# Moving the recurrent mixer and the index selection of a hybrid encoder block between the groups of its input projection

## The chip, the cores and the metric

The kernel runs on one core of a Trainium2 chip. The metric is device time in microseconds for one launch, the median of three runs. A separate execution was profiled, and all durations below come from it.

## What is computed

One block of a hybrid encoder, in float32, for 256 tokens of width 2048:

```
h = h + 0.5 * swiglu(rms_norm(h), w_gate, w_up, w_down)          # FFN 1, d_ff 5632
u = rms_norm(h) @ w_in
q, k, v, qi, ki, wi, rr, rk, rv, wd, ad, gd = split_columns(u)
attn = dsa_attention(rope(q), rope(k), v, rope(qi), rope(ki), wi)
rwkv = rwkv7_time_mix(rr, rk, rv, wd, ad, gd, ...)
h = h + concat([attn, rwkv]) @ w_out
h = h + 0.5 * swiglu(rms_norm(h), ...)                           # FFN 2
return rms_norm(h)
```

The attention has 8 heads of 128. An indexer scores every key (8 small heads, relu, weighted sum), keeps the 64 best of each query under a chunk-causal mask, and the softmax runs over those. The recurrent half has 16 heads of 64. For each head and each time step it does

```
sa = state @ a_t
state = state * w_t + sa b_t^T + v_t k_t^T
y_t = state @ r_t
```

followed by a normalisation within heads, a bonus term and a gate.

## The kernel before

**Projections.** Weights stream through four slots. One group is 256 rows by 512 columns of a weight matrix (512 KB). SP issues its load into `raw` once the slot's earlier group has been split. ACT copies it to the rounded high part `whi` (`split_hi`, L279), DVE subtracts to get the low part `wlo` (`split_lo`, L288), and TensorE multiplies high by high, low by high and high by low (`project_tokens`, L303, or `project_channels`, L631, in the input projection). A split waits until TensorE has used the group four places earlier. Every engine runs its own list in order, so an operation that stands between two splits delays the later one. The groups of the middle part are numbered from the start of the input projection: 0 to 7 are its small columns, 8 to 87 its ten chunks of 512 columns, eight groups each. The output projection has four chunks of eight groups.

**The mixer during the input projection.** `win_dve`, `win_act` and `win_pe` list the splits and matmuls of groups 8 to 87, with the elementwise preparation of the recurrent half placed between them: `in_out(c)` scales a finished chunk out of PSUM, `lerp` mixes each token with its predecessor, then come the decay (a cumulative sum and two exponentials), the key norm, and the transposes to token order. Two PSUM pairs (`psA`, `psB`) take the chunks in turn, the other two (`psT`, `psM`) the small rounds. A round is filled by TensorE and read by DVE or ACT; `fill`, `full`, `stored` are its semaphores.

**The mixer after the input projection.** `systems_*` and `rwkv_*` follow, all before the output projection:
1. Within each chunk of 64 tokens the recurrence is a triangular system. TensorE forms the systems (`bx`, `kx`, L1405), DVE masks them.
2. The 32 by 32 diagonal blocks go to DRAM and come back with one block per partition. DVE inverts them by substitution, 31 steps of two instructions (`tinv`, `subst`). The inverses go back over DRAM (L1549 to L1557), and TensorE combines them to 64 by 64 (L1446, L1454, with copies by ACT between).
3. The index scores and the selection of 64 keys on DVE (`scores_dve`: eight pairs of `max` and `match_replace` for each half of the queries, L866).
4. `akv`, `sa0` and the state maps `gt` (L1432, L1468), then the scan over four chunks: solution `sa` (L1488), output `ys` (L1508, L1509), next state `st` (L1517, L1518), each read by DVE or ACT before the next. Logits, softmax and attended values (L943, L952, L961) stand between the scan's rounds.
5. The normalisation (L1354, L1345, L1338), bonus and gate, then the high and low parts for the output projection.

The weight buffers `raw`, `whi`, `wlo` hold mixer tensors in this part (`bx` lies in `whi`, `kx` in `wlo`, `att` in `raw`), so no weights can be split meanwhile. The residual `x` stays in SBUF throughout.

Of the kernel before, what the change touches and what calls it, by code (L numbers as in the profile page):

```python
# [17 lines left out]
F32 = mybir.dt.float32  # L18
# [5 lines left out]
P = 128  # L24
# [73 lines left out]
def build(nc, a, out):  # L98
    with ExitStack() as ctx:
# [48 lines left out]
        ar = at("ar", [P, 2, NT, S], arena, 0)  # L148
        kk, r = ar[:, 0, :, :], ar[:, 1, :, :]
        k, v = at("k", [P, NT, S], arena, 2), at("v", [P, NT, S], arena, 3)  # L150
        temp = at("temp", [P, 5, S], arena, 7)
        qk = at("qk", [P, 10, S], arena, plus=61 * KB)
        vals = at("vals", [P, TB, S], arena, plus=71 * KB)
        qi = at("qi", [P, 5, S], arena, plus=73 * KB)
        lora = at("lora", [P, 2, S], arena, plus=78 * KB)
        lora_w = at("lora_w", [P, RW], arena, plus=80 * KB)
        lora_g = at("lora_g", [P, RW], arena, plus=84 * KB)
        small_tok = at("small_tok", [P, TB, 320], arena, 5)
        mix_hi_at = (at("mix_hi0", [P, NT, S], arena, 0, dt=F32R), at("mix_hi1", [P, NT, S], arena, 1, dt=F32R))
        mix_lo_at = (at("mix_lo0", [P, NT, S], arena, 6, dt=F32R), at("mix_lo1", [P, NT, S], arena, 4, dt=F32R))  # L160
        rows_of = at("rows_of", [P, TB, P], arena, 5, 4 * KB)
        token_scale = sb("token_scale", [P, S])
        widx_scale = sb("widx_scale", [P, TB])
        widx = sb("widx", [P, TB, IDX_HEADS])

        att = (at("att0", [P, AH, P], raw, 1, 4 * KB), at("att1", [P, AH, S], raw, 0))
        turned = at("turned", [P, AH, S], raw, 0)
        relu = (at("relu0", [P, IDX_HEADS, P], stage, 0), at("relu1", [P, IDX_HEADS, S], raw, 0))
        prob_t = at("prob_t", [P, TB, AH, P], xl, 1)
        score = at("score", [P, TB, S], arena, 7)  # L170
        top8 = at("top8", [P, 8], arena, 7, 2 * KB)
        top = [at(f"top{i}", [P, 3 * AH], arena, 7, 2 * KB + 64 + 96 * i) for i in range(TB)]

        ksq = at("ksq", [P, NT, S], arena, 3)
        sw = at("sw", [P, NT, S], arena, 4)
        pdec = at("pdec", [P, NT, S], arena, 4)
        lsum = at("lsum", [P, NT, S], arena, 5)
        pinv = at("pinv", [P, NT, S], arena, 5)
        bonus = at("bonus", [P, NT, S], arena, 5)
        iclr = at("iclr", [P, NT, S], arena, 6)  # L180
        gate = at("gate", [P, NT, S], xh, 1)
        hstat = at("hstat", [P, 3, S], stage, plus=4 * KB)
        ka1 = sb("ka1", [P, NT])
        pend = sb("pend", [P, NT * NCHUNK, 1])

        a_tok = at("a_tok", [P, TB, RW], arena, 3)
        v_tok = at("v_tok", [P, TB, RW], arena, 4)
        b_tok = at("b_tok", [P, TB, RW], arena, 0)
        k_tok = at("k_tok", [P, TB, RW], arena, 6)
        bx = at("bx", [P, 2 * RH, 2, C], whi)  # L190
        kx = at("kx", [P, 2 * RH, 2, C], wlo)
        tt_all = at("tt_all", [P, 2 * RH, C], arena, 2)
        nsys = at("nsys", [P, 1024], arena, 10)
        tinv = at("tinv", [P, 1024], arena, 10, 4 * KB)
        subst = at("subst", [P, 1024], stage, 0, 4 * KB)
        t_plain = at("t_plain", [P, 2 * RH, 32], raw, 1)
        xm = at("xm", [P, 2 * RH, 32], arena, 9, KB)
        akv = at("akv", [P, TB, RW], xl, 1)
        sa0 = at("sa0", [P, TB, RW], stage)
        gt = at("gt", [P, TB, RW], arena, 3)  # L200
        state = at("state", [P, NT, C], arena, 10)
        sdec = at("sdec", [P, NT, C], arena, 10, 2 * KB)
        sa = at("sa", [P, RW], arena, 10, 4 * KB)
        y = at("y", [P, NT, S], arena, 2)
        ysq = at("ysq", [P, NT, S], arena, 3)
# [41 lines left out]
        a_rest = sem("a_rest")  # L247
        lora_landed = sem("lora_landed")
        round_full = sem("round_full")
        round_read = [sem(f"round_read{i}") for i in range(4)]  # L250
        sys_stored = sem("sys_stored")
# [96 lines left out]

        def turn_x(f, c):
# [5 lines left out]
            if c >= 2 or f:  # L355
                nc.tensor.wait_ge(xl_ready, DC * f + c - 1)
            if f == 0 and c == 1:
                nc.tensor.wait_ge(params_ready, 1)
            ps = (psT, psM)[c % 2]
# [6 lines left out]
        def x_hi(f, c):  # L366
# [3 lines left out]
            ps = (psT, psM)[c % 2]  # L370
# [6 lines left out]
        def x_lo(f, c):  # L377
            nc.vector.wait_ge(xh_ready, DC * f + c + 1)
            ps = (psT, psM)[c % 2]
# [148 lines left out]
        def ffn_pe(f, base):  # L528
# [11 lines left out]
            def chunk(n, first):  # L540
# [3 lines left out]
                for j in range(GD):  # L544
                    if first and j % 2 == 0:
                        if f == 0:
                            for q in ((0, 1), (2,), (3,), ())[j // 2]:
                                turn_x(0, q)
                        elif j == 2:
                            turn_x(2, 3)  # L550

                        nc.tensor.wait_ge(xl_ready, 4 * (2 * f) + j // 2 + 1)
                    project_tokens(psA, xh, xl, base, n, PER, j, j * KT, j == 0, j == GD - 1)
                if not first:
                    turn(n - 1)
                elif f == 0:
                    turn_params()
# [1260 lines left out]
```

## Time and profile before

| | |
|---|---|
| median of 3 runs | 2056.07 us (2054.09 to 2060.73) |
| profiled execution | 2050.65 us, its span 2048.8 us |
| TensorE / DVE / ACT / POOL busy | 1965.0 / 1070.0 / 835.4 / 8.2 us |
| mean granted clock of TensorE | 0.968 |
| DMA | 349.37 MB, mean 171 GB/s |

Busy time is the union of an engine's instructions; matmuls are pipelined, so a busy TensorE isn't one at its peak. A float32 matmul of the small rounds is recorded as two matmuls, a rounded one (fp32r) as one. The chain of waits is followed back from the last instruction, at each step to what released it.

### The profile page before, as it was taken

The numbers are of one execution on the slowest core, as the hardware profiler recorded it, in microseconds if no ns is written. First come the engines' busy times: TensorE is split into PE (matmuls) and PEld (weight loads), VectorE is DVE, ScalarE is ACT, GpSimd is POOL, SyncE is SP. The second block draws the span as 40 slices with busy tenths as digits, with TensorE's granted clock in tenths as the row PEclk, the third lists the DMA queues.
The fourth block names the chain that finished last, engine by engine and source line by source line (L and its number), as shares of the span: only waits on it lengthen the run. The fifth ranks groups of instructions, "written<-read, shape, count | busy, mean of one in ns | idle before, by whom it ended". The sixth has DMA issues, their size and how long they took to land.

```text
span 2048.8 us, 28872 instructions
## 1 busy us (share of the span) xinstructions
PE 1965.0 (96%) x10849; PEld 1674.5 (82%) x10849; DVE 1070.0 (52%) x1104; ACT 835.4 (41%) x947; POOL 8.2 (0%) x20
## 2 busy tenths in 40 slices
PE   7999999999999999999965989999999999999997
PEld 5888888888888889999955868888888888888886
DVE  4444544554544445787575275545454554444443
ACT  5444444444344445423321234544444444444443
POOL 1000000000000000000000000000000000000000
PEclk9999999999999999999985689999999999999999
DMA  6666666666666666546401026666666666666663
GB/s 199 188 191 188 191 189 190 185 192 187 192 189 192 192 190 191 157 141 185 134 22 37 1 93 205 183 209 191 189 192 187 191 187 186 192 187 195 195 194 125
DMA packets 192742, 349.37 MB, mean 171 GB/s; under 512 B 23632, under 2 KB 25936, under 8 KB 192400
## 3 DMA queue, kind: packets, MB, share of 16 engines
q1 hardware_dynamic: 191968, 348.04, 57.0%
q8 instruction: 60, 0.98, 0.2%
q14 instruction: 26, 0.21, 0.0%
q0 software_dynamic: 512, 0.06, 0.0%
q10 hardware_dynamic: 176, 0.07, 0.0%
HBM read 344.46 MB, written 3.67 MB: 170 GB/s over the span
## 4 chain that ended last, share of the span: by engine, by line
PE 94%; DVE 3%; DMA 1%; ACT 1%; issue 1%; SPq 0%; ACTq 0%; DVEq 0%
PE psA L303 38%; PE psB L303 37%; PE psA L631 6%; PE psB L631 5%; PE psT L536 1%; PE psB L642 1%; DVE tinv L817 1%; DVE subst L817 1%; PE psT L1338 0%; PE psT L363 0%; DVE wlo L288 0%; DMA raw<-in_w_in 0%; DVE qk L817 0%; PE psM L1338 0%; ACT xh L374 0%
## 5 line engine op out<-in xcount | busy, mean ns | idle before, releaser
L288 DVE TENSOR_TENSOR wlo<-raw,whi 128x1024 fp32r<-128x1024 f32 (+1 forms) x648 | 788.5, 1219 | 846.7 <-ACT whi L279 844.0
L279 ACT CAST whi<-raw 128x1024 fp32r<-128x1024 f32 (+1 forms) x648 | 677.1, 1047 | 1001.6 <-PE psA L303 443.0
L303 PE MATMUL psA<-whi,xh 128*128 128x512 f32 (+1 forms) x736 | 285.4, 388 | 8.3 <-DVE wlo L288 8.3
L303 PE MATMUL psA<-whi,xl 128*128 128x512 f32 (+1 forms) x736 | 284.7, 387 | 0.0
L303 PE MATMUL psA<-wlo,xh 128*128 128x512 f32 (+1 forms) x736 | 284.4, 386 | 0.0
L303 PE MATMUL psB<-whi,xh 128*128 128x512 f32 x704 | 275.7, 392 | 0.0
L303 PE MATMUL psB<-whi,xl 128*128 128x512 f32 x704 | 274.0, 389 | 0.0
L303 PE MATMUL psB<-wlo,xh 128*128 128x512 f32 x704 | 274.0, 389 | 0.0
L303 PEld LDWEIGHTS psA<-whi,xh 128*128 128x128 f32 x736 | 139.3, 189 | 37.0 <-issue 7.1
L303 PEld LDWEIGHTS psA<-wlo,xh 128*128 128x128 f32 x736 | 139.4, 189 | 27.7
L303 PEld LDWEIGHTS psA<-whi,xl 128*128 128x128 f32 x736 | 139.1, 189 | 27.9
L303 PEld LDWEIGHTS psB<-whi,xl 128*128 128x128 f32 x704 | 132.2, 188 | 27.5
L303 PEld LDWEIGHTS psB<-wlo,xh 128*128 128x128 f32 x704 | 132.3, 188 | 26.8
L303 PEld LDWEIGHTS psB<-whi,xh 128*128 128x128 f32 x704 | 132.2, 188 | 26.8
L303 PE MATMUL psA<-whi,hh 128*128 128x512 f32 x352 | 137.2, 390 | 0.0
L303 PE MATMUL psB<-whi,hh 128*128 128x512 f32 x352 | 137.1, 389 | 0.0
L303 PE MATMUL psA<-whi,hl 128*128 128x512 f32 x352 | 137.0, 389 | 0.0
L303 PE MATMUL psA<-wlo,hh 128*128 128x512 f32 x352 | 136.9, 389 | 0.0
L303 PE MATMUL psB<-whi,hl 128*128 128x512 f32 x352 | 136.9, 389 | 0.0
L303 PE MATMUL psB<-wlo,hh 128*128 128x512 f32 x352 | 136.9, 389 | 0.0
L631 PE MATMUL psA<-xh,whi 128*128 128x256 f32 x320 | 91.2, 285 | 0.0
L631 PE MATMUL psA<-xh,wlo 128*128 128x256 f32 x320 | 90.5, 283 | 0.0
(371 smaller groups left out, 2271.2 us busy)
## 6 DMA issues: line engine op xcount, KB each, us to landing
raw<-in_ffn_w_gate SPq DMA_DIRECT2D x176, 512.0 KB, 3.7
raw<-in_ffn_w_up SPq DMA_DIRECT2D x176, 512.0 KB, 3.6
raw<-in_ffn_w_down SPq DMA_DIRECT2D x176, 512.0 KB, 4.1
raw<-in_w_in SPq DMA_DIRECT2D x80, 512.0 KB, 3.7
raw<-in_w_out SPq DMA_DIRECT2D x32, 512.0 KB, 4.1
x<-in_x SPq DMA_DIRECT2D x4, 512.0 KB, 7.4
out<-x SPq DMA_DIRECT2D x4, 512.0 KB, 4.2
raw<-in_w_in SPq DMA_DIRECT2D x8, 192.0 KB, 2.9
```

What stands on the lines that cost most here:

```text
L279: nc.scalar.copy(whi[:, slot, :, 0:ncol], raw[:, slot, :, 0:ncol]).then_inc(hi_ready, 1)
L288: nc.vector.tensor_tensor(wlo[:, slot, :, 0:ncol], raw[:, slot, :, 0:ncol], whi[:, slot, :, 0:ncol].bitcast(F32), ALU.subtract).then_inc(l ...
L303: mm = nc.tensor.matmul(ps[:, tb, 0:ncol], lhs[:, k0 + t, tok], rhs[:, slot, t, 0:ncol], start=(first and t == 0 and p == 0), stop=(last a ...
L536: mm = nc.tensor.transpose(psT[:, t * S + tb * P:t * S + tb * P + P], act[:, tb, t * P:t * P + P], ident)
L631: mm = nc.tensor.matmul(ps[:, i * S:(i + 1) * S], w[:, slot, t, ct * P:(ct + 1) * P], h[:, k0 + t, :], start=(first and t == 0 and p == 0 ...
L642: mm = nc.tensor.matmul(ps[:, at + tb * step:at + tb * step + width], h[:, k0 + t, tok], w[:, slot, t, col:col + width], start=(first and ...
L817: return V.tensor_tensor(out, a0, a1, op)
```

## The change

The mixer's work after the input projection is spread over the groups of that projection, and the layout of memory is changed.

- The mixer tensors leave `raw`, `whi` and `wlo`. They lie in the arena (the feed-forward part's hidden values), in `stage`, and in `x`, whose contents are written to DRAM after load 11 (`spill_x`) and read back behind eight loads of the output projection (`reload_x`).
- The chunks come in another order: index queries 7, queries 8 and 9, keys and values last (10). Queries and index queries are no longer scaled by the token's norm in `in_out`: ACT copies them, and the scale is folded into `widx_scale` and `att_scale`.
- The systems are formed in four pairs of rounds (`b0`, `k0`, `b1`, `k1`) of 64 columns; 128 columns before. The state is kept as decayed at the chunk's end, with two buffers. `b_end` and `k_end` fall away.
- Triangle, combination, `akv`, `sa0`, `gt`, index scores, selection and scan get places between groups 38 and 87. After the projection remain variance, gate, logits, softmax, attended values and the gated output.
- POOL zeroes the inverse and its target. ACT computes `kk_raw`, its square and the transposed inverse.
- The output projection takes its first two chunks by halves: attention rows of both, then recurrent rows of both.
- At the kernel's start the third block of `x` is turned into `psB`, the fourth into `psT`, and both earlier in TensorE's list.

The core of the diff:

```diff
+        def turned_in(f, c):
+            if f == 0 and c >= 2:
+                return (psB[:, :, :].rearrange("p b c -> p (b c)"), psT)[c - 2]
+            return (psT, psM)[c % 2]
...
                     if first and j % 2 == 0:
                         if f == 0:
-                            for q in ((0, 1), (2,), (3,), ())[j // 2]:
-                                turn_x(0, q)
+                            if j == 0:
+                                turn_x(0, 0)
+                                turn_x(0, 1)
+                                turn_x(0, 2)
...
+                    if first and f == 0 and j == 1:
+                        turn_x(0, 3)
...
+        def mix_load(sp):
+            load_small(sp)
+            load_in(sp, GD, 12)
+            spill_x(sp)
+            load_in(sp, 12, 47)
+            store_system(sp)
+            load_in(sp, 47, 48)
+            load_system(sp)
+            load_in(sp, 48, 67)
+            store_inverse(sp)
+            load_in(sp, 67, 68)
+            load_inverse(sp)
+            load_in(sp, 68, 84)
+            load_gate(sp)
+            load_in(sp, 84, NCH * GD)
+            load_out(sp, 0, 8)
+            reload_x(sp)
+            load_out(sp, 8, DC * GD)
```

In `win_dve`, where `splits(a, b)` are the low splits of groups a to b-1:

```diff
+            splits(50, 51)
+            mask_dve("k1", kx1, 1)
+            splits(51, 52)
+            in_out(5)
+            substitute(9, 11)
+            splits(52, 53)
+            lerp_chunk(5)
+            splits(53, 54)
+            substitute(11, 14)
+            splits(54, 55)
+            substitute(14, 17)
+            splits(55, 56)
+            substitute(17, 20)
+            splits(56, 57)
+            substitute(20, 24)
+            splits(57, 58)
+            substitute(24, 31)
+            splits(58, 59)
+            in_out(6)
+            lerp_chunk(6)
+            splits(59, 61)
...
+            scan_state(2)
+            splits(82, 83)
+            scan_y(2)
+            scan_sa(3)
+            splits(83, 84)
+            top_dve(1, 2, 4)
+            splits(84, 85)
+            V.wait_ge(in_read, 10)
+            rope_q(1)
+            splits(85, 86)
+            top_dve(1, 4, 8)
+            splits(86, 88)
+            scan_y(3)
```

In `win_pe`:

```diff
+            win_groups(72, 73)
+            for i in range(2):
+                stored(T, "b1", i)
+                stored(T, "k1", i)
+            scan_y_pe(0)
+            index_pe(2)
+            win_groups(73, 74)
+            index_pe(3)
+            scan_sa_pe(1)
+            win_groups(74, 76)
+            scan_state_pe(1)
+            win_groups(76, 77)
+            scan_y_pe(1)
+            win_groups(77, 78)
+            scan_sa_pe(2)
+            win_groups(78, 80)
+            scan_state_pe(2)
+            win_groups(80, 81)
+            scan_y_pe(2)
+            win_groups(81, 82)
+            scan_sa_pe(3)
+            win_groups(82, 84)
+            scan_y_pe(3)
+            win_groups(84, 86)
+            for c in range(NCHUNK):
+                stored(T, "ys", c)
+            within_heads("mean", y)
+            win_groups(86, NCH * GD)
```

**SP's queue, from the loads ahead of chunk 1.** The names: `raw` are weights, `n_dram` and `t_dram` the blocks on their way through DRAM. Before:

```order
L614 DMA lora_g<-in_rwkv_g 64x1024
L268 DMA raw<-in_w_in 128x2x512 x80
L1543 DMA n_dram<-bx 32x32x32 x4
L1546 DMA nsys<-n_dram 128x1024
L1549 DMA t_dram<-subst 128x1024
L1550 DMA t_dram<-tinv 128x1024
L1554 DMA tt_all<-t_dram 32x32x32
L1557 DMA t_plain<-t_dram 32x32x32
L1554 DMA tt_all<-t_dram 32x32x32 x2
L1557 DMA t_plain<-t_dram 32x32x32
L1554 DMA tt_all<-t_dram 32x32x32
L268 DMA raw<-in_w_out 128x2x512 x32
```

And with the change:

```order
L279 DMA raw<-in_w_in 128x2x512 x4
L651 DMA x_dram<-x 256x1x512 x4
L279 DMA raw<-in_w_in 128x2x512 x35
L667 DMA n_dram<-bx_102 32x32x32 x4
L279 DMA raw<-in_w_in 128x2x512
L672 DMA nsys<-n_dram 128x1024
L279 DMA raw<-in_w_in 128x2x512 x19
L676 DMA t_dram<-tinv 128x1024
L678 DMA t_dram<-subst 128x1024
L279 DMA raw<-in_w_in 128x2x512
L686 DMA t_plain<-t_dram 32x32x32
L688 DMA tt_all<-t_dram 32x32x32 x2
```

The trip through DRAM stood behind all 80 loads and now stands in four places among them, and the residual's store behind the fourth load. Three more inverse loads, 16 weight loads, the gate weights, four weight loads, eight of the output projection and the residual's return follow.

**DVE, the end of the triangle.** `wlo` rows are splits. Before:

```order
L817 TENSOR_TENSOR subst<-nsys,tinv 128x60
L817 TENSOR_TENSOR tinv<-tinv,subst 128x2x30
L817 TENSOR_TENSOR subst<-nsys,tinv 128x31
L817 TENSOR_TENSOR tinv<-tinv,subst 128x31
L1189 MEMSET tt_all 128x2048
L1190 COPY subst<-tinv 128x1024
L858 TENSOR_SCALAR score<-relu_70,widx 128x128
L860 SCALAR_TENSOR_TENSOR score<-relu_70,widx,score 128x128 x7
```

And with the change:

```order
L922 TENSOR_TENSOR tinv<-tinv,subst 128x2x30
L922 TENSOR_TENSOR subst<-nsys,tinv 128x31
L922 TENSOR_TENSOR tinv<-tinv,subst 128x31
L299 TENSOR_TENSOR wlo<-raw,whi 128x1024
L922 TENSOR_TENSOR v<-psA,token_scale 128x1024
L922 TENSOR_TENSOR temp<-v 128x4x255
L1110 TENSOR_SCALAR temp<-v 128x4
L1112 SCALAR_TENSOR_TENSOR v<-temp,pcol,v 128x256 x4
L299 TENSOR_TENSOR wlo<-raw,whi 128x1024 x2
L922 TENSOR_TENSOR bonus<-bonus,v 128x2048
```

The last steps were followed by the index scores; now a split, the scaling and mixing of chunk 6 and two splits stand there, and the zeroing and the turned copy have left DVE.

**TensorE, ahead of the output projection.** `prob_t,vals` are the attended values, `hstat` the norm factors. Before:

```order
L952 MATMUL psB<-consts,att_68 128x128 x8
L952 MATMUL psA<-consts,att_68 128x128 x8
L1354 MATMUL psT<-y,consts 128x512 x2
L1354 MATMUL psM<-y,consts 128x512 x2
L961 MATMUL psB<-prob_t,vals 128x512 x4
L1345 MATMUL psT<-ysq,consts 16x256 x8
L1338 MATMUL psM<-hstat,consts 128x256 x4
L1338 MATMUL psT<-hstat,consts 128x256 x4
L303 MATMUL psA<-whi,mix_hi_62 128x512
```

And with the change:

```order
L1544 MATMUL psT<-lora_gs,lora_g 128x256 x4
L1544 MATMUL psM<-lora_gs,lora_g 128x256 x4
L1067 MATMUL psT<-kr,q 128x128 x8
L1067 MATMUL psM<-kr,q 128x256 x4
L1067 MATMUL psT<-kr,q 128x256 x4
L1552 MATMUL psM<-hstat_gn,consts 128x256 x4
L1552 MATMUL psT<-hstat_gn,consts 128x256 x4
L1076 MATMUL psM<-consts,att_105 128x128 x8
L1085 MATMUL psT<-prob_t,vals 128x512 x2
L1076 MATMUL psM<-consts,att_106 128x128 x8
L1076 MATMUL psT<-consts,att_106 128x128 x8
L1085 MATMUL psM<-prob_t,vals 128x512 x4
```

The rounds of gate and logits, which stood earlier, now come behind the variance round that ends the projection's groups, and the attended values are last.

## Rows read from the trace of the kernel before

**Rows 1.** The page: TensorE's busy time, its slices, its clock, ACT's split of weights
```profile
PE 1965.0 (96%) x10849; PEld 1674.5 (82%) x10849; DVE 1070.0 (52%) x1104; ACT 835.4 (41%) x947; POOL 8.2 (0%) x20
...
PE   7999999999999999999965989999999999999997
...
PEclk9999999999999999999985689999999999999999
...
L279 ACT CAST whi<-raw 128x1024 fp32r<-128x1024 f32 (+1 forms) x648 | 677.1, 1047 | 1001.6 <-PE psA L303 443.0
```

**Rows 2.** Chain that ended last: start us, us, what; the start, then 1029 to 1351
```profile
34.51 12.77 PE psA L303 x48
...
1029.67 1.24 DVE qk L817
...
1096.04 3.46 PE psA L1446 x61
...
1196.14 3.45 PE psB L961 x8
...
1214.26 24.45 PE psA L303 x96
...
1329.35 21.76 PE psB L303 x96
```

**Rows 3.** Waits, 0 to 100 and 1029 to 1216 us: total, times, longest
```profile
PE psA L303 <- DVE wlo L288: 8.3, 3, 4.6
...
PE psA L1446 <- DMA tt_all<-t_dram: 39.5, 1, 39.5
```

**Rows 4.** Stretches: us, busy us (x instructions) by engine, granted clock, DMA share, GB/s
```profile
762.00:771.00 9.00, 7.20 (x60) 6.98 (x58) 4.96 (x10) 6.48 (x12) 0.00 (x0) 1.00 0.99 314
...
1000.00:1029.00 29.00, 29.00 (x245) 29.00 (x243) 10.07 (x9) 7.33 (x7) 0.00 (x0) 1.00 0.28 83
...
1060.00:1075.00 15.00, 0.00 (x0) 0.00 (x0) 13.73 (x38) 2.19 (x3) 0.00 (x0) 0.50 0.00 1
```

**Rows 5.** Chain that ended last, input projection: its first and last piece
```profile
771.16 7.51 PE psB L631 x48
...
1006.60 23.05 PE psA L631 x192
```

**Rows 6.** TensorE's forms (busy us, mean ns, idle before), then single rounds by time
```profile
L1432 PE MATMUL psT<-v_tok,kx 64*64 64x64 f32 x64 | 2.1, 220 | 0.0
...
L1468 PE MATMUL psT<-tt_all,a_tok 64*64 64x64 f32 x64 | 3.4, 220 | 0.0
...
L1362 PE MATMUL psA<-consts,iclr 128*128 128x128 f32 x8 | 1.1, 280 | 0.0
...
1129.03 0.19 PEld L1508 LDWEIGHTS psT<-bx,sa 64*64 64x64 f32 x2 [0.33 <-issue]
...
1132.41 0.19 PEld L1517 LDWEIGHTS psM<-sa,b_tok 64*64 64x64 f32 x2
...
1138.03 1.72 PE L1488 MATMUL psT<-state,gt 64*64 64x64 f32 x29
```

**Rows 7.** DVE by time: first, tenth and last step of the triangle
```profile
1059.38 0.19 DVE L817 TENSOR_TENSOR subst<-nsys,tinv 128x31 f32<-128x31 f32 x1
...
1065.28 0.39 DVE L817 TENSOR_TENSOR subst<-nsys,tinv 128x220 f32<-128x220 f32 x1
...
1082.52 0.19 DVE L817 TENSOR_TENSOR tinv<-tinv,subst 128x31 f32<-128x31 f32 x1
```

**Rows 8.** DVE's forms, 790 to 1030 (first row) and 1029 to 1216 us
```profile
L288 DVE TENSOR_TENSOR wlo<-raw,whi 128x1024 fp32r<-128x1024 f32 x72 | 87.9, 1225 | 69.2 <-ACT whi L279 68.6
...
L866 DVE MAX8 top<-score 128x8 f32<-128x256 f32 x8 | 3.4, 427 | 0.3
...
L1256 DVE TENSOR_SCALAR y<-y,pcol 128x256 f32<-128x256 f32 x4 | 1.4, 407 | 0.0
...
L879 DVE TENSOR_REDUCE top<-att 128x8 f32<-128x2048 f32 x1 | 2.3, 2286 | 0.0
```

More of the change, by code:

```diff
@@ L167, in build @@
[L167 to L176, printed above, removed]
@@ L189, in build @@
[L189 to L198, printed above, removed]
@@ new lines, in scan_sa, with scan_state @@
+        def scan_sa(c):
+            half, blk = c % 2, c // 2
+            hp = slice(64 * half, 64 * half + 64)
+            ps = full(V, "sa", c)
+            vread(tt(sa[hp, :], sa0[hp, blk, :], ps[hp, :], ALU.add), "sa", c)
+        def scan_state(c):
+            ps = full(V, "st", c)
+            s3 = ps[:, 0:COLS].rearrange("p (t v) -> p t v", v=C)
+            new, old = states[c % 2], states[(c + 1) % 2]
+            ends = pend[:, c:32:4, :].to_broadcast([P, NT, C])
+            if c == 0:
+                vread(tt(new[:, :, :], s3, ends, ALU.mult), "st", 0)
+            else:
+                vread(tt(new[:, :, :], old[:, :, :], s3, ALU.add), "st", c)
+                vdone(tt(new[:, :, :], new[:, :, :], ends, ALU.mult), f"state{c}")
@@ new lines, in win_act @@
+            splits(70, 72)
+            for i in range(2):
+                copy_tokens("sa0", sa0, i)
+            splits(72, 73)
+            for i in range(2):
+                copy_tokens("gt", gt, i)
+            splits(73, 74)
+            index_act(0)
+            index_act(1)
+            in_out_act(8)
+            splits(74, 76)
+            scan_y_act(0)
+            index_act(2)
+            splits(76, 77)
+            index_act(3)
+            splits(77, 80)
+            scan_y_act(1)
@@ L1470, in rwkv_pe, with sa_of, scan_sa_pe @@
                 filled(mm)
+        def sa_of(c):
+            return sa0[:, 0, :] if c == 0 else sa[:, :]
+        def scan_sa_pe(c):
+            half, blk = c % 2, c // 2
+            hs = slice(64 * half, 64 * half + 64)
+            state = states[(c - 1) % 2]
+            if c == 1:
+                stored(T, "st", 0)
+            else:
+                need(T, f"state{c - 1}")
+            ps = fill("sa", c)
+            for jj in range(RH):
+                par, t = jj // NT, jj % NT
+                ch = slice(64 * par, 64 * par + 64)
+                mm = T.matmul(ps[hs, jj * C:(jj + 1) * C],
+                              gt[ch, blk, half * COLS + t * C:half * COLS + (t + 1) * C], state[ch, t, :],
+                              start=True, stop=True)
+            filled(mm)
```

1201 lines of the change are left out of this document (654 added, 547 removed), and 10 rows, old and new, of tables (late, rounds).

## The prediction

> **What bounds the kernel now.** I read the page's totals and slices first, then the chain of work that ended last, the stretches by engine, the waits, and last single instructions. TensorE is busy 1965.0 us of 2048.8 [rows 1]; nearly everywhere the next group of weights is used the moment the last one ends. The slices show the exception: near the middle TensorE's digits fall to 6, 5 and 8 and the granted clock to 5, 6, 8. The chain puts a place to it [rows 2]. The input projection ends at 1029.67 us, the output projection begins at 1214.26, and the 184.6 us between are a relay: a DVE triangle, a round trip through DRAM, small TensorE rounds, DVE additions. TensorE waits 39.5 us in one piece for the inverted blocks, then for one DVE or ACT step after another [rows 3]; between 1060 and 1075 it does nothing, and the clock it is granted there is half [rows 4]. The weights of the output projection can't hide this, since their product needs the mixed heads. So the time is bounded by TensorE in the projections and by latency in this stage. In the projection DVE needs 1.23 us and ACT about 1.05 for a group that costs TensorE 24 matmuls, 2.88 us (258.5 us from 771.16 to 1029.67, small rounds included) [rows 1, 2, 5, 8]: there is the room for the moved work.
>
> **What stays as it was.** The two feed-forward parts and the output projection keep their matmuls. Its chunks 0 and 1 take attention halves first, which alone needs no earlier data, as the program lets it start after the last attended round. I cost it at nothing.
>
> **TensorE's sum.** The 258.5 us of the projection keep their small rounds. What moves in, at the full clock:
> - akv and sa0: 64 matmuls each, 64 by 64, adjacent ones on different halves of the rows. A round of 64 records takes 1.86 to 2.0 us [rows 6], so four rounds 7.9. The two state-map rounds, whose neighbours share rows, take 3.0 each: 6.0 [rows 6].
> - The four systems become 256 matmuls of 64 columns (before, as many records at 128). By the alternating rate 16.0 us, by the other 24; their rows change at every second matmul, and I take 18, since the alternating rows are nearest.
> - Combining the blocks: 4 rounds of 3.46 or less at half clock [rows 2] become about 6.4 in all.
> - The scan. Its first output round takes 3.6 us (1129.03 to 1132.4), a state round 3.6 (to 1136.0), a solution round 1.7 [rows 6]. So 3 x 1.7 + 3.6 + 3 x (1.7 + 3.6) + 3 x 3.6 = 35.4.
> - Index scores 2.6, four transposed rounds at 0.9 (busy 1.0 with their overlap [rows 6]), two of the means at 1.7: 9.6.
> Sum: 7.9 + 6.0 + 18 + 6.4 + 35.4 + 9.6 = 83.3 us. The Trainium skill (TensorE: Matmul & The Clock Gate, "The mechanism" of Part 3) says a weight load overlaps a running matmul only when the row group differs; by it every second matmul of the systems pays the dear rate and they cost 20, not 18. The trace agrees with the rule on akv against the state maps, 1.9 against 3.0 us.
>
> **Where DVE and ACT can't follow.** Both split each group before TensorE may use it, in queue order, at most four groups ahead; every moved operation stands between two splits. I added up each stretch between TensorE's end of one group and the split it needs later.
> - Triangle: its 62 instructions take 23.3 us, 5.9 of them the first nine steps, 17.4 the other 22 [rows 7]. From TensorE's end of group 47 DVE has: 1.1 waiting for ACT, 9 splits 11.1, 17.4, two scaled chunks 2.5, two lerps of 3.4 (one operation of 1.2, four of 0.48, one of 0.17): 38.9. TensorE has eleven groups and two turned rounds, 31.7 + 3.5 = 35.2, until it wants group 59. Stall 3.7.
> - End of the scan: from the last solution round DVE has 1.2, five splits 6.1, six pairs of top-8 at about 0.95 (0.43 the first of a pair [rows 8]), the rotation of half the queries 5.6, a sum 0.7: 19.4. TensorE has four groups and an output round, 16.8. Stall 2.6.
> - Elsewhere DVE's load is below TensorE's. Groups 43 to 50, for one: 8 splits 9.8 and 21.5 of other work against 23.0 and 13 of rounds.
> - The DRAM trip now stands in SP's queue between loads: four stores after load 46, one load back, two stores after load 66, six loads after 67. TensorE wants the inverse only after group 64, some 18 us later. SP is held about 5 us at group 68, whose split waits for group 64 anyway: hidden. If the cover is gone, 5 us.
> - Spilling the residual puts 2 MB into the queue after load 11, where the queue is fullest: 314 GB/s from 762 to 771 [rows 4], so 6.7 us. Three raw groups stand ahead; I take 1. The gate weights leave the same place, 0.25 MB at that rate: -0.8. The way back (2 MB) is issued behind eight output loads, while DVE and ACT work in the tail: 0.
> - Zeroing the inverse moves from DVE to POOL, which only waits for the first statistic: 0. The key products' squares move to ACT: 0.
> Stalls 3.7 + 2.6 + 1 - 0.8 = 6.5.
>
> **The tail.** Behind the last projection group stand only statistics, keys and values, logits, softmax, normalisation. DVE holds the path: it waits for the statistic (4.0), scales the last chunk and rotates the keys (4.5), one split and the reciprocal (3.0), two blocks of logits with their maxima (three at 1.22, 1.2, 2.3 [rows 8]: 7.2), normalises half (three at 1.22, four at 0.41 [rows 8]: 5.3), one probability 1.3, the other half 5.3, one low part 1.2, the second probability 2.4: 34.2. Then transposes 2.2 and copies 1.0, the attended round 3.45 [rows 2], ACT 1.0, DVE 1.2: 43. With the clock near half, where TensorE idled, the last rounds double and give 49; I take 47.
>
> **Start.** The third and fourth blocks of x are turned before groups that need them, in other banks, instead of between groups. TensorE waits 8.3 us for DVE's splits in the first 100 us [rows 3]; the chain enters group 4 at 34.51 [rows 2], where after the change group 2, at 21.6, is followed by two more at 2.8: 27.3. Gain 7.2; between 0 and 8, and I take it since x's last block waits for no TensorE work then.
>
> **Sum.** New end of the projection 1029.7 + 83.3 + 6.5 - 7.2 = 1112.3; output projection from 1159.3 instead of 1214.3; 55.0 less. Its first groups run at the falling clock's pace as before (24.45 against 21.76 [rows 2]). The profiled execution took 2050.65 us; it would take 1995.7. The median shown is 5.4 above it: 2001.
>
> Bounds: no stall at all -7, start not gained +7, systems -2 or +6, tail 40 to 55: -7 or +8. Moved rounds may each also wait for DVE or ACT: the scan's waits before on one step were up to 1.8 us on a DVE addition; over 15 rounds, 27.
>
> **The rivals.**
> 1. *Coupled queues.* DVE, ACT and TensorE each hold projection groups behind a dependent step. Every round then adds a short wait, up to the 27 above, and the time is 2028. For it: 62 dependent instructions on DVE and ten scan rounds now stand in one queue with splits. Against: three groups, 8.6 us, of cover, and DVE idle 69.2 us of the old projection [rows 8]. Chance 0.2.
> 2. *Clock lost, slower.* Micro-waits among small rounds bring TensorE to its 1.2 GHz level. About 343 us of TensorE work stand in the new stage; at half clock a share f of it adds 343 f. It decides from f = 0.16; at f = 0.25 the time is 2001 + 86 = 2087. For it: in the old relay the level was half between 1060 and 1075 though work came in bursts. Against: the old projection ran at 1.00 with its small rounds inside, from 1000 to 1029 for one [rows 4]. Chance 0.04. The Trainium skill (TensorE: Matmul & The Clock Gate, "A second HAM failure mode: psum-queue depth-cycling") names just this, short idling between groups making the clock swing; no row here shows it where groups keep coming.
> 3. *The cover isn't there:* the residual's two ways and the DRAM trip hold the loads: 6.7 + 6.7 + 5 more, 2019. Chance 0.1.
> That the change doesn't do what it says is excluded by the order of the queues.
>
> **Numbers.** My case 0.66, predicted 2001. Range 1985 to 2032: below, the bounds of stalls, tail and systems; above, rivals 1 and 3. 0.3% of 2056 is 6 us, about what a measurement of this kernel can tell. Faster by more 0.94, within 0.02, slower 0.04 (rival 2).
>
> **What would show it.** Output projection beginning near 1159; TensorE's granted clock 1.00 from 771 to 1110, half near 1140; a TensorE wait on wlo of some 4 us near group 59 and one for the mean round of some 3; no wait for DMA after 780; the start's wait of 8.3 nearly gone. The prediction fails if the projection lasts much over 350 us, or the tail over 55.

## The result, and the profile after the change

| | before | after |
|---|---|---|
| median, us (lowest to highest, 4 runs each) | 2055.08 (2045.56 to 2060.73) | 1988.3 (1986.76 to 1989.08) |
| profiled execution, its span, us | 2050.65, 2048.8 | 1986.76, 1985.0 |
| granted TensorE clock, mean | 0.968 | 0.988 |
| input projection from its group 8 to its end, us | 258.5 | 342.0 |
| from there to the output projection, us | 184.6 | 50.7 |

The ratio is 0.9679, with an interval of 0.9642 to 0.9716: 66 us faster. I had predicted 2001 within 1985 to 2032, and 55 us. The runs of the kernel before spread over 15 us and those of the kernel after over 2. Of the 12.7 us between 2001 and 1988.3, 8.9 are in the profiled execution (1995.7 predicted, 1986.76 found); the rest is the 5.4 that I added to come from the profiled execution to the median, which is only 1.5 above it now.

The page after, TensorE's totals, then the slices of TensorE and of its clock (tenths):

```profile
PE 1939.5 (98%) x11105; PEld 1646.5 (83%) x11105; DVE 1049.0 (53%) x1098; ACT 849.4 (43%) x964; POOL 11.0 (1%) x23
...
PE   8999999999999999999999799999999999999997
...
PEclk9999999999999999999999799999999999999998
```

Where [rows 1] had three weak slices and a clock that fell to half, there is one slice at 7. The first slice rose from 7 to 8: that is the start.

Stretches of after (us, then busy us and instructions of PE, PEld, DVE, ACT and POOL, granted clock, DMA share, GB/s): the input projection from group 8, what stands between it and the output projection, the larger part of that alone, and the first output groups:

```profile
758.57:1100.57 342.00, 334.21 (x3899) 319.38 (x3900) 233.46 (x347) 141.19 (x162) 2.86 (x3) 0.99 0.48 144
1100.57:1151.25 50.68, 33.38 (x118) 21.08 (x117) 33.79 (x38) 19.13 (x44) 0.00 (x0) 0.73 0.19 63
...
1116.00:1151.00 35.00, 19.41 (x54) 10.58 (x52) 22.45 (x25) 14.53 (x40) 0.00 (x0) 0.66 0.11 41
1151.00:1175.00 24.00, 23.75 (x98) 19.59 (x99) 8.72 (x8) 7.43 (x8) 0.00 (x0) 0.93 0.43 131
```

The projection holds 342.0 us, 83.5 more than [rows 5] gave it, and TensorE is busy in 334.2 of them at a clock of 0.99. DVE, at 10.07 us of 29 in the last stretch of [rows 4], is at 233 of 342: the triangle and the additions now stand here, under TensorE's work. The rest of the old relay is the 50.7 us of the second row, where the clock still falls, to 0.66 over the last 35.

TensorE's waits between 740 and 1180 us (total, times, longest):

```profile
PE psM L1076 <- DVE att L922: 8.8, 2, 6.8
PE psB L730 <- DVE wlo L299: 4.8, 4, 2.3
PE psM L1568 <- DVE y L922: 3.0, 1, 3.0
```

The 39.5 us for the inverse in DRAM [rows 3] are gone and no DMA took their place. Rows two and three are the two lags of DVE that the prediction named: of the 4.8 us of row two 4.1 stand ahead of groups 58 and 59 (1.8 and 2.3), the other 0.7 ahead of groups 8 and 12; row three is 3.0 (predicted 3.7 and 2.6). The first row is the tail.

The chain that ended last, in order of time (start us, us, what). The start:

```profile
11.09 1.97 PE psB L382 x8
13.05 6.20 PE psA L314 x24
19.26 0.87 PE psT L382 x8
20.13 16.37 PE psA L314 x72
```

The third block of x is turned at 11.09, ahead of the groups, the fourth at 19.26; then nothing stops TensorE, where [rows 2] entered a group at 34.51 behind waits of 8.3 [rows 3]. The place of the second DVE lag, and the tail:

```profile
1091.16 1.96 PE psM L1568 x4
...
1100.57 3.57 PE psM L1559 x16
...
1126.83 1.98 PE psM L1076 x8
...
1130.05 3.77 PE psT L1085 x4
...
1138.62 1.98 PE psT L1076 x8
...
1141.84 6.60 PE psM L1085 x8
1148.44 2.81 issue
1151.25 12.69 PE psA L314 x48
```

The tail is a relay in small as before, with its rounds at half the clock: eight transposes take 1.98 us, an attended round 3.77 and 6.60.

### The profile page after: what moved, and what is told of

It reads as the page before. It is cut to its first block, busy times and chain, and to the rows that moved or that the text cites. A ratio compares the mean times of both kernels' runs of the same rounds, so it can differ in the third digit from the quotient of the medians.

```text
span 1985.0 us, 29402 instructions
## 1 busy us (share of the span) xinstructions
PE 1939.5 (98%) x11105; PEld 1646.5 (83%) x11105; DVE 1049.0 (53%) x1098; ACT 849.4 (43%) x964; POOL 11.0 (1%) x23
## 4 chain that ended last, share of the span: by engine, by line
PE 93%; DVE 4%; DMA 1%; ACT 1%; issue 1%; SPq 0%; ACTq 0%; DVEq 0%
PE psA L314 39%; PE psB L314 38%; PE psB L730 5%; PE psA L730 4%; PE psT L555 1%; DVE wlo L299 1%; DMA raw<-in_w_in 1%; DMA x<-in_x 0%; DVE subst L922 0%; PE psM L1085 0%; DVE tinv L922 0%; PE psA L741 0%; PE psT L1067 0%; ACT whi L290 0%; DVE y L922 0%
## 5 line engine op out<-in xcount | busy, mean ns | idle before, releaser
L730 PE MATMUL psB<-xh,whi 128*128 128x256 f32 x320 | 93.5, 292 | 4.8 <-DVE wlo L299 4.8
L730 PE MATMUL psB<-xh,wlo 128*128 128x256 f32 x320 | 91.2, 285 | 0.0
```

The lines of the kernel that those rows point to most:

```text
L730: mm = nc.tensor.matmul(ps[:, i * S:(i + 1) * S], w[:, slot, t, ct * P:(ct + 1) * P], h[:, k0 + t, :], start=(first and t == 0 and p == 0 ...
```

## The experiments

Twelve kernels; each changes the kernel after by the lines shown, unless it says otherwise. The medians of before in their four groups of runs were 2048.94, 2048.4, 2046.44 and 2047.93.

**The start alone, and all but the start.** The one turns the blocks of x in the new order in the kernel before, the other puts the old order back in the kernel after. The second edit, in part:

```
-            if f:
+            if c >= 2 or f:
                 nc.tensor.wait_ge(xl_ready, DC * f + c - 1)
-            elif c == 3:
-                nc.tensor.wait_ge(xl_ready, 1)
...
-                            if j == 0:
-                                turn_x(0, 0)
-                                turn_x(0, 1)
-                                turn_x(0, 2)
+                            for q in ((0, 1), (2,), (3,), ())[j // 2]:
+                                turn_x(0, q)
```

> The changed kernel with the old order of turning x at the start. Theory: the new order is worth the 10.8 us by which the small groups of the input projection begin earlier (745.9 against 756.7 us), and nothing downstream absorbs it, so the time rises from 1988.3 to about 1999. Rival: the residual's store behind load 11 makes the first full groups wait for DMA (759.3 to 769.6 us on the chain), and would be hidden if the start were later; then part is given back and the time is about 1992.

> The kernel before with the new order of turning x alone. Theory: the two parts add, 2055.1 - 10.8 = 2044.3 us; the input projection of the kernel before then waits for its first loads as before. Rival: that DMA wait (5.8 us on the chain at 763 to 769) grows when the work in front of it ends earlier, and less than 6 us remain: 2049 or more.

Old order in the new kernel: 1998.71 us, 10.4 more; new order in the old kernel: 2039.26, 9.7 less by the medians, 7 by the ratio of 0.9964, whose interval, 0.9934 to 0.9994, spans 1 to 14 us. The medians can't tell more than that the two agree roughly. The traces tell it more closely: the small groups of the input projection begin 9.8 us later with the old order in the new kernel (755.68 against 745.91) and 9.2 us earlier with the new order in the old one (747.51 against 756.71). So the start adds to the rest and interacts with it by a microsecond at most up to there. All but the start is worth 50 us (1998.71 against 2048.94). With the old order TensorE's wait in the first 100 us is the one of [rows 3] again, and at the same size:

```profile
PE psA L314 <- DVE wlo L299: 8.3, 3, 4.6
```

With the new one, in either kernel, no wait for DVE is left there. The gain is somewhat more than the 8.3 us of the wait; the part on the prediction says why.

**What the systems' rounds cost, by their order.** Two kernels change only the loops of the four systems. In the kernel neighbouring matmuls differ in the column half, or in column and row half, by turns, so that four quarters of the array take turns.

```
-                for t in range(NT):
-                    for par in range(2):
+                for par, half in ((0, 0), (0, 1), (1, 0), (1, 1)):
+                    for t in range(NT):
...
```

> The changed kernel with the eight rounds of the systems in another order of matmuls: row half and column half fixed over eight matmuls in a row, same work. Each round of 64 records takes 1.09 and 0.93 us now. Theory: they are fast because neighbours use other quarters of the array; with the quarter fixed a round takes 3.0 us, as the state maps do, 16 us more TensorE work in all, and the time rises by 12 to 16 us (DVE waits at some of them). Rival: their inputs and 64 columns alone set the rate, a round stays near 1.0 and the time at 1988.

```
-                for t in range(NT):
-                    for par in range(2):
+                for par in range(2):
+                    for t in range(NT):
```

> The systems' rounds with the half of the rows outermost and only the half of the columns alternating from matmul to matmul (in the kernel both change, so that four quarters take turns: 1.1 us for 64 records; all fixed: 3.4). Theory of the quarters: two quarters take turns, which is half as fast as four, about 1.8 to 2.0 us a round, as akv's diagonal pair; 8 rounds cost 6 to 7 us more than 9.2, profile 1994. Rival, only a change of rows hides the load: 3.4 a round as with all fixed, about 2001.

One line per form of the first two rounds (duration of a record, then first and last start): after, all in one quarter, rows kept and columns alternating:

```profile
L1589 PE MATMUL psM<-kk,iclr x64: 217/218/268, 863.7 to 864.7; 64*64 64x64 f32 x64
L1589 PE MATMUL psT<-kk,iclr x64: 217/218/219, 864.7 to 865.6; 64*64 64x64 f32 x64
```
```profile
L1588 PE MATMUL psM<-kk,iclr x64: 218/218/267, 862.1 to 865.3; 64*64 64x64 f32 x64
L1588 PE MATMUL psT<-kk,iclr x64: 218/218/267, 865.1 to 868.3; 64*64 64x64 f32 x64
```
```profile
L1589 PE MATMUL psM<-kk,iclr x64: 218/218/267, 863.1 to 864.8; 64*64 64x64 f32 x64
L1589 PE MATMUL psT<-kk,iclr x64: 218/218/267, 864.6 to 866.3; 64*64 64x64 f32 x64
```

A record lasts 218 ns in all three; what differs is how many run beside each other. Sixty-four records start in 1.0 us with four quarters in turn, in 3.2 with one and in 1.7 with two. The times follow, each from a single execution: 2001.82 with one quarter (15.0 us more of span, four pairs of rounds by 4.3 us are 17.1), and 1989.34, a span of 1987.5, with two (2.5 more; four pairs by 1.3 are 5.1, of which TensorE's waits for the low parts, 2.7 in place of 4.8, give back 2.1). So a change of the column half alone brings a round from 3.2 to 1.7 us, and the second kernel refutes its rival, 3.4 us a round, outright. A change of the row half alone stands in no run. The profiled time of 1994 was not reached: the rounds cost 5 us more and not 6 to 7, and slower rounds gave DVE's lag some of its time.

**The triangle's last steps later.**

```
-            substitute(24, 31)
+            substitute(24, 25)
             splits(58, 59)
...
-            splits(59, 61)
+            splits(59, 60)
+            substitute(25, 31)
+            splits(60, 61)
```

> DVE's triangle steps 25 to 30 moved from ahead of the split of group 58 to behind that of group 59. Theory: the two waits of TensorE on the low part of the weights near 941 and 946 us, 4.3 us together, are DVE's lag behind a triangle that is issued in one lump; six of the last steps (about 5 us of DVE) moved behind one more split and the lerp let TensorE run through, and the inverse, which goes through DRAM, is wanted only some 20 us later. Expected 1984, no wait there. Rival: the lag is only shifted by a group or two and TensorE waits as long behind group 60: 1988.

Measured 1986.91 (1986.08 to 1989.29), 1.4 less, with runs that overlap those of the kernel after (1986.76 to 1989.08). The rival holds. In the kernel after, the wait's place in the chain is this:

```profile
937.50 0.31 DVE tinv L922
...
939.86 1.22 DVE wlo L299
941.08 1.14 DVE v L922
...
943.99 1.28 DVE v L1112 x3
945.29 1.23 DVE wlo L299
...
946.57 4.53 PE psB L730 x24
```

With the steps moved the waits become this:

```profile
PE psB L730 <- DVE wlo L299: 4.0, 3, 2.9
...
PE psM L1617 <- DMA tt_all<-t_dram: 0.7, 1, 0.7
```

DVE is behind by a sum, not by a lump: with six steps moved behind two more splits TensorE waits 0.9 us ahead of group 59 and 2.9 ahead of group 60, one group later and 3.7 together instead of 4.1, and the inverse's way through DRAM begins to show at its end, 0.7 us. The cover predicted for that way is real, and short.

**The last of the top-8 search in the tail.**

```
-            splits(85, 86)
-            top_dve(1, 4, 8)
-            splits(86, 88)
+            splits(85, 88)
...
             out_split_lo(2)
+            top_dve(1, 4, 8)
```

> The last four pairs of DVE's top-8 search and the bias moved from ahead of the split of group 86 to the tail, ahead of the reading of the variance, where DVE waits 4.0 us for TensorE. Theory: TensorE's wait of 3.0 us ahead of the mean round goes, the 4.0 us of search fill the wait in the tail, and 1988.3 becomes 1985. Rival: the search delays the keys' rotation and the logits by what the wait doesn't cover, since the variance round then comes 3 us earlier too: 1988.

Measured 1982.42 (1978.23 to 1984.04), 5.9 less: more than the theory's 3. The mean round waits for nothing, TensorE going straight on from a group that ends at 1085.85:

```profile
1085.85 1.72 PE psM L1567 x4
1087.57 1.72 PE psT L1567 x4
```

The rest can be read in the profiled execution, which with 1978.23 is the fastest of the six and 8.5 less than that of the kernel after, so the pieces add up to more than the medians differ by. TensorE's waits for the low parts are 3.3 instead of 4.8, the tail is shorter by 1.5, and the first output groups come at 11.17 us for 48 instead of 12.69: the clock is granted at 1.00 over them, at 0.85 over the same time in the kernel after. Why it is back sooner is not shown. Here the work did fill a hole: DVE waited 4 us in the tail for a statistic.

**Idle matmuls in the tail, to keep the clock.** They write a bank that nothing reads.

```
+        def keep_clock(n):
+            for i in range(n):
+                T.matmul(pA[:, 0:COLS], ident, consts[:, 0:COLS], start=True, stop=True)
...
+            keep_clock(12)
             turn_probabilities_pe(0)
+            keep_clock(1)
             attend_pe(0)
+            keep_clock(8)
             turn_probabilities_pe(1)
             attend_pe(1)
+            keep_clock(5)
```

> The changed kernel with 26 idle float32 matmuls of 128 by 512 (52 records) added into psA where TensorE waits in the tail, results unused: 12 before the first transposed probabilities, 1 before the first attended round, 8 before the second transposes, 5 behind the last attended round. Theory: the clock there is granted at 0.66 because TensorE idles; kept at full, the last attended round takes 3.5 instead of 6.6 us, the first one 1.8 instead of 3.8, transposes half, and the output projection starts at its full pace: 6 to 9 us less, about 1981. Rival: the filling delays rounds on TensorE's queue as much as it saves, and the time stays within 2 us of 1988.

> As the filled tail, with fewer idle matmuls: 5 ahead of the first transposed probabilities, 1 ahead of the attended round, 4 ahead of the second, 3 at the end (12, 1, 8 and 5 before). Theory: the filled tail gained nothing because its filling ran on for 6.6 us after the probability was ready, 2 to 3 us in the second gap and 1.5 in the third, which gave back what the full clock brought to the rounds (attended rounds 1.95 and 3.67 us against 3.77 and 6.60, turned ones 0.89 against 1.98, first output groups 10.9 against 12.7: 8.8 together). With a filling cut to the gaps 6 to 9 us remain: 1979 to 1982. Rival, the clock doesn't come back with so little filling, or the gaps are DVE's anyway: 1985 to 1990.

With 26 of them 1989.78, no gain. With 13 it was 1984.28 (1981.69 to 1985.84), 4.0 less. The chain of the first and then of the second:

```profile
1124.49 12.54 PE psA L1799 x24
1137.02 0.89 PE psM L1076 x8
...
1141.10 6.87 PE psA L1799 x16
```
```profile
1140.91 1.11 PE psT L1076 x8
...
1143.25 5.19 PE psM L1085 x8
...
1151.26 11.16 PE psA L314 x48
```

The clock does come back (eight transposes in 0.89 us), but the twelve matmuls of the first gap ran to 1137.02, while the probability they were to bridge to would have been there some 6 us earlier (in the smaller filling it comes 6.3 us after the gap's start). Cut to size, the filling gives about half of what I expected (6 to 9): the tail takes 48.2 us instead of 50.7, the first 48 matmuls of the output projection 1.5 less. The rest of the chain in this stretch is then DVE without a break from 1115.13 to 1140.86: the half clock had hidden that the tail is bound by DVE's queue.

**The scan's heads in another order.** I wanted neighbours to change quarter in the state maps and the scan too. The edit, at five places (four in the second kernel, which keeps the solution rounds):

```
-            for jj in range(RH):
+            for jj in (0, 4, 1, 5, 2, 6, 3, 7):
```

> The state-map rounds and all ten scan rounds take their eight heads in the order 0, 4, 1, 5, ... so that neighbouring matmuls lie in another half of the rows, of the columns, or of both (before: four heads in a row in one quarter). Theory of the quarters: the systems' rounds took 1.1 us for 64 records when neighbours changed quarter and 3.4 when they kept it, the diagonal rounds of akv 2.0, so matmuls in different quarters run beside each other, whether rows or columns differ. By it the scan's rounds halve (state 3.6 to 1.8, solution 1.8 to 0.9, output 5.4 to 2.7: 35.4 to 17.7) and the two state maps go from 3.2 to 1.2 each. 21.7 us of TensorE work less; of it 3 to 6 go into longer waits for DVE at the end of the scan, so 1988.3 becomes 1970 to 1973. Rival, rows alone matter: only the solution rounds (2.7 less), the first part of three output rounds (2.8 less) and the state maps (3 to 4 less) gain: 1979 to 1981. Rival, the accumulating pairs of the state and output rounds, both to one address, hold each other up whatever the neighbour does: as the second, 1979 or more.

> As the alternating scan, but the three solution rounds keep their old order (four heads in a row on the same half of the rows); state maps, state rounds and output rounds alternate. In the solution rounds all eight heads write the same half of PSUM's partitions, and neighbours that differ in rows alone would write the same columns of the array's output together; in the others neighbours write different halves. Theory: what the alternating scan computed otherwise came from that, and its time from the others: 3 x 0.8 us comes back, 1975. Rival: neighbours that accumulate in two halves of one bank disturb each other, so state and output rounds are the ones that computed otherwise; the time is the same 1975 then, the sums tell it.

Measured 1972.69 and 1972.5. Neither says anything on the theory, and the trace shows why. State rounds of after, and of the first of the two:

```profile
L1671 PE MATMUL psM<-sa,b_tok x64: 218/218/268, 1007.9 to 1057.5; 64*64 64x64 f32 x64
```
```profile
L1671 PE MATMUL psM<-sa,b_tok x32: 218/218/267, 1004.8 to 1045.0; 64*64 64x64 f32 x32
```

Half the records. There are sixteen heads, eight to each half, not eight; my list runs over the first eight only, all of them in one quarter. So these kernels leave half of the heads out of the maps and the scan, and nothing in them alternates. The expectations' words on "what the alternating scan computed otherwise" rest on the same mistake. What the time does tell: leaving out half of it, 21 of 42 us, brought 15.7, so here TensorE's time is still the kernel's for the most part; the wait ahead of the mean round grew from 3.0 to 4.3, and two of 1.2 and 0.9 us came behind DVE's additions and splits.

**All that helped, and then the quarters.** The first takes the late search, an attention-first tail and six idle matmuls in its gaps (1, 2, 1, 2).

```
-            normalised_dve(0)
-            probabilities_dve(0)
-            normalised_dve(1)
-            rwkv_lo(0)
-            probabilities_dve(1)
-            rwkv_lo(1)
-            attended_lo(0)
-            attended_lo(1)
+            spread_dve(0)
+            probabilities_dve(0)
+            spread_dve(1)
+            probabilities_dve(1)
+            attended_lo(0)
+            normalised_dve(0)
+            normalised_dve(1)
+            attended_lo(1)
+            rwkv_lo(0)
+            rwkv_lo(1)
```

(`spread_dve` is the first line of `normalised_dve`, which reads the bank; ACT's queue has both copies of the mixed half behind the attended ones.)

> Three edits outside the scan together: the last four pairs of the top-8 search in the tail; in the tail DVE and ACT do both probabilities and the attended low parts ahead of the normalisation and gate of the recurrent half, which the output projection reads only eight groups (23 us) after its start; and six idle matmuls in the gaps of TensorE (1 ahead of the first attended round, 2 and 1 in and behind the second turned pair, 2 at the end). Theory: the tail's length is DVE's queue and the half clock of six rounds. From 1982.4 with the search alone, the first probability comes 4 us earlier, the second turned round 6.5 us earlier at equal clock, and the full clock gives 3 to 5 more: 1970 to 1973. Rival: ACT's and DVE's normalisation, 14 us of it now beside the first output groups, makes their splits late and TensorE waits there instead: 1977 or more.

Measured 1971.29 (1968.25 to 1971.5), ratio 0.961 (0.9583 to 0.9636): faster than before and than after. The tail, from its chain that ended last:

```profile
1119.99 1.97 PE psM L1076 x8
1121.96 1.71 PE psA L1804 x2
1123.66 2.20 PE psT L1087 x4
1125.86 0.88 PE psM L1076 x8
...
1130.69 3.67 PE psM L1087 x8
...
1137.53 11.17 PE psA L314 x48
```

From the variance round at 1097.47 to the output projection 40.1 us, against 50.7. TensorE waits for no split behind it, so the rival falls: the normalisation fits under the first output groups.

The second has every state round, and the second part of every output round, go from one half of the columns to the other at each matmul:

```
-            for jj in range(RH):
-                par, t = jj // NT, jj % NT
-                ch = slice(64 * par, 64 * par + 64)
-                out_ = ps[ch, t * C:(t + 1) * C]
+            for t in range(NT):
+                for first in (True, False):
+                    for par in range(2):
+                        jj = par * NT + t
+                        out_ = ps[64 * par:64 * par + 64, t * C:(t + 1) * C]
...
```

> The same with state maps, state rounds and output rounds of the scan alternating strictly from one half of the columns to the other at every matmul, so that no two neighbours lie in one half (before they came in pairs that accumulate, both in one half); the solution rounds keep their order. Theory: what those rounds computed otherwise came from a pair in one half beside work in the other, and strict turns compute what the kernel computes. TensorE has 19 us less, of which DVE's lag at the end of the scan and near group 59 gives back 3 to 4: 15 us less than the version it is built on, 1956. Rival: accumulation itself disturbs a neighbour in the other half; the time is the same, the sums tell it. Rival: DVE, whose work doesn't shrink, bounds the last groups: 5 to 8 us given back, 1960 or more.

Measured 1955.47 (1955.17 to 1957.22). These rounds have all their heads; but the state maps and the first parts of three output rounds still went by the list above, with half the heads, so this isn't a kernel to use. Its whole rounds are worth reading (the second state round, its first and last start, after and here):

```profile
L1671 PE MATMUL psT<-sa,b_tok x32: 217/218/268, 1031.3 to 1034.7; 64*64 64x64 f32 x32
```
```profile
L1678 PE MATMUL psT<-sa,b_tok x32: 218/218/267, 1026.4 to 1028.2; 64*64 64x64 f32 x32
```

The same records in 1.8 us instead of 3.4, as the systems' rounds with alternating columns had shown. From [rows 6] on, 3.6 us was the price of an order, not of the work. What a kernel with the complete lists would take was not run. My estimate is a microsecond more than this one: full maps at the 1.7 to 1.9 us of alternating columns take what the halved ones take in one quarter (3.3 us for both, from 994.55 to 997.88), and the first parts would lie on diagonal quarters, as akv's.

## Why the prediction was right, and which of its terms were off

The likeliest case came about: TensorE's time in the projection plus two lags of DVE, the rest hidden. The output projection begins at 1151.25; predicted was 1159.3, from 1214.26. The 8 us between are these.

- **Start.** Predicted 7.2 less. The small groups that open the input projection come 10.8 us earlier than before, and both exchange experiments give 9 to 10. The term was sized by one piece of the chain up to group 4, and the bound of 8 by the wait that the profile lists; both fell short. The trace has the rest. Group 4 begins at 25.6 (24 of the 72 matmuls behind 20.13), where I had put it at 27.3: 8.9 us earlier than at 34.51. And the four groups from there, which came behind the waits at a granted clock of 0.87, now run at 1.00, 1.9 us less. Before, then after:

```profile
34.51:47.28 12.77, 12.77 (x49) 10.18 (x49) 7.50 (x8) 11.10 (x20) 0.00 (x0) 0.87 0.76 220
```
```profile
25.60:36.51 10.91, 10.91 (x50) 8.82 (x48) 6.98 (x8) 10.21 (x19) 0.00 (x0) 1.00 0.78 225
```

- **First loads of the projection.** Group 8 gains 1.8 more: TensorE's wait ahead of it was 2.0 us before and is 0.2. I had put 0.8 of that down to the gate weights, which left the fullest queue [rows 4]. The exchange kernels separate start and loads: with the old loads and the new start the wait is 0.7, with the new loads and the old start there is none. Which of the moved loads does it is not separated. The spilled residual costs 0.5 at group 12 (1).
- **Systems.** Predicted 18, bounds 16 to 24; they took 8.1, 2.0 for each pair of rounds. The start left its bounds too, but this is by far the larger miss. I had priced them by akv's alternating rate [rows 6], and that row has two quarters in turn where the systems have four; its neighbours change rows and columns at once, so it could not tell which of the two matters. A nearer row was the systems' own in the kernel before: eight rounds of 32 records of 128 columns, rows kept and columns alternating, 11.6 us from 1030.95 to 1042.54 for the same products. The second round:

```profile
L1405 PE MATMUL psB<-ar,iclr x32: 269/269/320, 1032.3 to 1034.0; 64*64 64x128 f32 x32
```

  The rule that a load is hidden only when the row group differs (the Trainium skill, TensorE: Matmul & The Clock Gate, "The mechanism" of Part 3) would give 20 here. The trace disagrees with it: rounds with the same rows and alternating columns took 1.7 us, not 3.2.
- **Combining rounds.** Predicted 6.4; two rounds of 2.14 us, 4.3. The 256 records are the old ones [rows 2], but each round now goes from one diagonal quarter to the other at every matmul, 17 ns apart; I had only allowed for the clock.
- **akv, sa0, maps, scan, scores.** Predicted 7.9, 6.0, 35.4 and 2.6; they took 7.8, 6.3, 35.9 and 3.2.
- **The moved work together.** 83.5 us more in the projection, of which waits are 0.5 at group 12, 4.1 at groups 58 and 59 and 3.0 at the mean: 75.9 of work against 83.3 predicted. Systems and combining rounds account for 12 us less, the line above for 1.3 more, so some 3 us came on top without a term. A tenth of a microsecond stands at each change between a group and a round; with some thirty such changes that would be most of it.
- **Stalls.** Triangle 4.1 (3.7), end of the scan 3.0 (2.6). The places were right. The exercise of adding up each stretch of DVE's queue against TensorE's told a lag of 3 to 4 us to within half a microsecond. The late search shows that the second was worth removing, the late triangle that the first doesn't go away when its steps move behind two more splits.
- **Tail.** Predicted 47 (43 at the full clock, 49 at half), 50.7 found. DVE's terms held: the second probability is there 35.3 us into the tail (34.2). The rounds at half clock cost more than the 6 us I gave them: by the rounds of the filled versions 1.1 more for each of two turned rounds, 1.8 and 2.9 for the attended ones, 6.9 in the tail, and 1.5 on the first output groups, 8.4 in all. And the last turned round waited another 1.7 us for DVE to empty its bank of the first attended values, which had no term. The reading that DVE holds the path there was right and became the best version's lever.

So the hit owes something to luck. Start, first loads, systems and combining rounds came in some 17 us under their terms, tail, stalls and moved rounds some 9 over; the 8 us are what is left of the two.

The rivals: *coupled queues* did not come, and none of the ten scan rounds is in the list of TensorE's waits; the groups ahead were cover enough. *Clock lost* did not come either: 0.99 over the whole projection. The oscillation that the Trainium skill describes (TensorE: Matmul & The Clock Gate, "A second HAM failure mode: psum-queue depth-cycling") doesn't appear where groups stand between the small rounds. After the wait of 3.0 us ahead of the mean round the clock differs from one execution to another: that round's two halves took 1.96 and 1.72 us at 1.00 in after, 3.75 and 2.99 at 0.50 and 0.59 in the run with 26 idle matmuls, which come behind it. *The cover isn't there* showed in nothing but the 0.5 us at group 12, and 0.7 for the inverse in the kernel with the late triangle.

## What to carry to other kernels

Latency-bound stages can be laid under a projection almost at the price of their TensorE records, if each dependent engine's queue is added up stretch by stretch; the places where it lags by a few microseconds come out of that sum. Price small matmuls by the order of the quarters that they occupy, since the same records cost 1.0, 1.7 or 3.2 us a round, and look whether the order can be changed before looking for a place to hide them. When a round's time halves at once, count its records before believing it.

## What was not expected of the hardware

- 64 records of 64 by 64 in float32, 218 ns each, start in 1.0 us with four quarters in turn (16 ns apart), 1.7 with two that share their rows, 3.2 in one (50 ns apart). Two that share neither rows nor columns took 1.9. I had expected that only a change of rows matters; no run has a change of rows alone.
- Six small idle stretches of TensorE in the tail, the longest 6.8 us, cost some 8.4 us by the clock (an estimate from the same rounds in the filled versions), and 13 matmuls that compute nothing won back 4.0 us of the median.
